# Three modulation tiles moved from the q and k projections to the v projections and the state updates

## The chip, the cores and the metric

The kernel runs on one core of a Trainium2 chip. The metric is the device time of one execution in microseconds (us), as the median of several runs; the kernel before has three runs, 2333.09, 2335.57 and 2336.96 us.

## The reference, cut to what matters

The model is one transformer block with a gated linear attention mixer and a mixture of experts, followed by a second block of other mixers and a plain MLP. The change touches only the beginning of the first block:

```python
mod_x = (jax.nn.silu(c) @ w_ada[l] + b_ada[l])[:, None, :]
sh1, sc1, g1, sh2, sc2, g2 = jnp.split(mod_x, N_MOD, axis=-1)
p_x = modulate(rmsnorm(h, norm_mix_w[l]), sh1, sc1) @ w_in[l]
p_c = modulate(rmsnorm(hc, norm_mix_w[l]), csh1, csc1) @ w_in[l]
# split p into q, k, v, gates, pool; chunked attention over context and tokens
h = h + g1 * (mix_x @ w_out[l])
h = h + g2 * moe(modulate(rmsnorm(h, norm_mlp_w[l]), sh2, sc2), ...)
```

There are 512 tokens and 256 context rows of width 1024. The modulation is a vector of 6 x 1024 values, cut here into 12 tiles of 512. Tiles 0 to 3 are sh1 and sc1 and are needed first. Tiles 4 to 7 are sh2 and sc2, needed only by the expert layer, after this phase. Tiles 8 to 11 are the gates g1 and g2.

## The kernel before, in words

`phase_first` is one block of five engine programs (SyncE, ScalarE, GpSimd, TensorE, VectorE), each a fixed list of instructions in written order, tied by semaphores. No planner chooses the order; it is the order of the calls in the file.

A modulation tile t takes four steps. SyncE loads a 2 MB piece of `w_ada` into a slot of the buffer `W` (`load`, recorded as L249). TensorE multiplies it with the silu of c in 32 small matmuls (`ada(t)`, L435) and raises `mm`. VectorE copies the 128x128 result to `mod_rows` (`row(t)`, L684), which raises `rowd`. TensorE turns it round by one transpose (`spread(t)`, L451), which raises `turn`, and VectorE adds the bias to it and stores it (`col(t)`, L697, and for scale tiles also L702), which raises `cold`. Tiles 4 to 11 all use the one slot 0, the one bank ps3 for `ada` and the one bank ps2 for `spread`. So `spread(t)` waits for `rowd` of t, `ada(t)` for `rowd` of t-1, `row(t)` for `turn` of t-1 and SyncE loads tile t only when `mm` has reached t, that is, when `ada(t-1)` has finished.

The projections are jobs: `project(j)` (L474) is eight matmuls of 512 columns (256 for the context half of k), into ps0 or ps1 in turn, and waits until the job two before it was taken out of its bank. Jobs 0 to 3 are the pool input, 4 to 7 are k (token and context parts), 8 and 9 are q, 10 to 15 are v for six tiles of rows, 16 to 19 are g. ScalarE takes jobs 4 to 15 out (`evict`, L332, semaphore `ev_a`), between large exponentials of the decay: in its order stand evict 4, evict 5, the exponential of `el` (L342), evict 6, two exponentials (L345, L347), evict 7. The exponential of `el` waits for four VectorE subtractions (L832), those of L345 and L347 for four more (L836). Job 8 cannot begin before evict 6, and job 9 not before evict 7.

VectorE's order there is: the scans of the decay (L824, L826), `row(5)`, the L832 subtractions, the L836 subtractions, `col(5)`, `row(6)`, `col(6)`, products with k (L844, L847), `row(7)`, `col(7)`, products with q (L853, L854), then `advance` for state steps 0 to 3 (L726). `update(step)` (L504) is 8 small TensorE matmuls, `turn_k` (L492) four transposes. The profile records each float32 matmul twice (16 for a job, 64 for an `ada`) and each transpose once. After job 15 come `ada(8)` and four rounds of job g, updates, scores, spread and the next `ada` (9 to 11); then the outputs and the projection `out` (L561), and the phase ends.

SyncE's own order matters too, because it is one queue:

```python
for t in range(5, 9):
    sp.wait_ge(mm, t)
    load(0, w_ada(t))
sp.wait_ge(zd, 1)
...
for i in range(fills):
    sp.dma_start(k.y[first + i * P:...], zero...).then_inc(zero_out, 16)
sp.wait_ge(pj, PROJ_V)
load(1, w_cols(a["w_out"], 0, 512))
for t in range(9, 12):
    sp.wait_ge(mm, t)
    load(0, w_ada(t))
```

The 15 fills (L275) write zeros of 512 KB each to `moe_y` in memory. They stand behind the load of tile 8, which waits for `ada(7)`, and ahead of half of `w_out` and of the load of tile 9.

Of the kernel before, what the change touches and what calls it, by code (L numbers as in the profile page):

```python
# [55 lines left out]
class Weights:  # L56
# [24 lines left out]
    def tile(self, n):  # L81
        kk, w = self.jobs[n][1]
        s = self.slot[n]
        return self.buf[:, s * SLOT:s * SLOT + kk * w].rearrange("p (k n) -> p k n", k=kk)
# [65 lines left out]
def phase_first(nc, k, a):  # L150
# [6 lines left out]
    with ExitStack() as st:  # L157
# [71 lines left out]
        def state(d, step):  # L229

            n = order[d][step] if step < NCH else None
            if n is None or n >= XCH:
                return S_ctx[:, step % 2, 2 * d:2 * d + 2, :]
            return S[:, n, 2 * d:2 * d + 2, :]
# [191 lines left out]
        def _(pe):  # L426
            def ada(t):
                pe.wait_ge(slot_in[ADA_HOME[t]], 16 * ADA_TURN[t])
                if 2 <= t < 4:
                    pe.wait_ge(rowd, t - 1)  # L430
                elif t >= 4:
                    pe.wait_ge(rowd, t)
                for kk in range(KD):
                    for q in range(4):
                        last = pe.matmul(ada_bank(t)[32 * q:32 * q + 32, :], narrow[:, kk, :], slot[ADA_HOME[t]][:, kk, tile(q)], start=kk == 0, stop=kk == KD - 1)  # L435
                last.then_inc(mm, 1)

            def spread(t):
                pe.wait_ge(rowd, t + 1)
                if 2 <= t < 4:  # L440
                    pe.wait_ge(cold, t - 1)
                elif t >= 4:
                    pe.wait_ge(cold, t)
                bank = spread_bank(t)
                if gate(t):
                    pe.wait_ge(picked, 5)
                    for q in range(4):
                        last = pe.matmul(bank[:, tile(q)], pick[:, q, :], modr[:, t % 2, :], start=True, stop=True)
                    last.then_inc(turn, 1)
                else:  # L450
                    pe.transpose(bank[:, 0:P], modr[:, t % 2, :], k.ident[:]).then_inc(turn, 1)  # L451
# [10 lines left out]
            def project(j, lo=0, hi=KD):  # L462
                lhs, rhs, n = jobs[j]
                if lo == 0:
                    if 2 <= j < 6:
                        pe.wait_ge(ev_v, j - 1)
                    elif 6 <= j < 18:
                        pe.wait_ge(ev_a, j - 5)
                    elif j >= 18:
                        pe.wait_ge(gmul, j - 17)  # L470
                for kk in range(lo, hi):
                    if j == 0:
                        pe.wait_ge(modx, 2 * kk + 2)
                    last = pe.matmul(ps[j % 2][:, 0:n], lhs(kk), rhs(kk), start=kk == 0, stop=kk == KD - 1)  # L474
                if hi == KD:
                    last.then_inc(pj, 1)
# [10 lines left out]
            def turn_k(n):  # L487
                i = STATE_TILES[n]
                if n >= 2:
                    pe.wait_ge(kdone, n - 1)  # L490
                for q in range(4):
                    last = pe.transpose(ps[4 + n % 2][:, tile(q)], el[:, q, tile(i)], k.ident[:])  # L492
                last.then_inc(tr, 1)

            def update(step):

                if step:
                    pe.wait_ge(sdone, 4 * step)
                for d in range(2):
                    n = order[d][step]  # L500
                    r = halfs[n % 2]
                    for h in range(4):
                        at = (h // 2) * P
                        last = pe.matmul(ps[6 + d][halfs[h % 2], at:at + P], el[r, 2 * d + h // 2, (n // 2) * P + 64 * (h % 2):(n // 2) * P + 64 * (h % 2) + 64],  # L504
                                         v[r, n // 2, h * P:(h + 1) * P], start=True, stop=True)
                last.then_inc(u, 1)
# [97 lines left out]
            spread(4)  # L604
            pe.wait_ge(slot_in[1], 32)
            project(4)
            ada(5)
            project(5)
            project(6)
            spread(5)  # L610
            ada(6)
            project(7)
            project(8)
            spread(6)
            ada(7)
            project(9)
            spread(7)
            pe.wait_ge(v_in, 32)
            project(10)
            project(11)  # L620
            pe.wait_ge(z_v, 1)
            pe.wait_ge(feat, 2)
            turn_k(0)
            turn_k(1)
            project(12)
            pe.wait_ge(kdone, 2)
            update(0)
            project(13)
            update(1)
            turn_k(2)  # L630
            turn_k(3)
            project(14)
# [44 lines left out]
        def _(dve):  # L677
            link = linker(dve, vch)

            def row(t):  # L680
                dve.wait_ge(mm, t + 1)
                if t >= 2:
                    dve.wait_ge(turn, t - 1)
                dve.tensor_copy(modr[:, t % 2, :], ada_bank(t)).then_inc(rowd, 1)  # L684

            def col(t):
                which, half = ADA_COLUMNS[t] // 2, ADA_COLUMNS[t] % 2
                dve.wait_ge(turn, t + 1)
                if gate(t):
                    dve.wait_ge(bg_in, 16 * (t - 7))  # L690
                    i, c = {2: 0, 5: 1}[which], slice(half * 512, half * 512 + 512)
                    dve.tensor_tensor(k.gate_rows[:, i, c], spread_bank(t)[:], bg[:], ALU.add).then_inc(cold, 1)
                    return
                i, f = {0: 0, 1: 1, 3: 2, 4: 3}[which], slice(half * 4, half * 4 + 4)
                src = spread_bank(t)[:, 0:P].rearrange("p (q a r) -> p q a r", q=4, a=2)[:, :, :, 0]
                bias = bcol[:, which * 8 + half * 4:which * 8 + half * 4 + 4].rearrange("p (q o) -> p q o", o=1).to_broadcast([P, 4, 2])
                dve.tensor_tensor(k.modc[:, i, f, :], src, bias, ALU.add).then_inc(cold, 1)  # L697
                if i in (1, 3):
                    name = "norm_mix_w" if i == 1 else "norm_mlp_w"
                    nw = k.vec[:, VEC[name] + half * 4:VEC[name] + half * 4 + 4].rearrange("p (q o) -> p q o", o=1).to_broadcast([P, 4, 2])  # L700
                    dve.wait_ge(cold, t + 1)
                    dve.scalar_tensor_tensor(out=k.modc[:, i, f, :], in0=k.modc[:, i, f, :], scalar=1.0, in1=nw, op0=ALU.add, op1=ALU.mult).then_inc(halfd, 1)  # L702
# [15 lines left out]
            def advance(step):  # L718
                dve.wait_ge(u, step + 1)
                if step >= 1:  # L720
                    dve.wait_ge(sdone, 4 * step)
                for d in range(2):
                    n = order[d][step]
                    for m in range(2):
                        at = m * P
                        dve.scalar_tensor_tensor(out=state(d, step + 1)[:, m, :], in0=state(d, step)[:, m, :], scalar=decay[:, 2 * d + m, n:n + 1],  # L726
                                                 in1=ps[6 + d][:, at:at + P], op0=ALU.mult, op1=ALU.add).then_inc(sdone, 1)
# [95 lines left out]
            for i in range(4):  # L823
                link(dve.scalar_tensor_tensor(out=cum[:, i, :], in0=cum[:, i, :], scalar=0.0, in1=el[:, i, :], op0=ALU.min, op1=ALU.subtract))  # L824
                back = slice(None) if i < 2 else slice(None, None, -1)
                dve.tensor_tensor_scan(cum[:, i, back], scanmask, cum[:, i, back], 0.0, ALU.mult, ALU.add).then_inc(cum_done, 1)  # L826
            row(5)
            dve.wait_ge(cum_done, 4)
            for i in range(4):
                lastp = 63 if i < 2 else 0  # L830
# [2 lines left out]
            for i in range(4):  # L833
                midp = 31 if i < 2 else 32
                cv = cum[:, i, 0:T].rearrange("p (n c) -> p n c", c=CH)
                dve.tensor_tensor(em[:, i, :].rearrange("p (n c) -> p n c", c=CH), cv, cv[:, :, midp:midp + 1].to_broadcast([P, XCH, CH]), ALU.subtract).then_inc(dm, 1)  # L836
            col(5)
            row(6)
            col(6)
            dve.wait_ge(ev_a, 4)  # L840
            dve.wait_ge(ee, 6)
            for d in range(2):
# [2 lines left out]
            for d in range(2):  # L845
                dd = slice(2 * d, 2 * d + 2)
                dve.tensor_tensor(ei[:, dd, :], ei[:, dd, :], kT[:, :, 0:T], ALU.mult).then_inc(feat, 1)  # L847
            row(7)
            col(7)
            dve.wait_ge(ev_a, 6)  # L850
            for d in range(2):
                dd = slice(2 * d, 2 * d + 2)
# [1 line left out]
                dve.tensor_tensor(cum[:, dd, 0:T], cum[:, dd, 0:T], qT, ALU.mult).then_inc(feat, 1)  # L854
            dve.wait_ge(zeroed, 2)
            dve.wait_ge(const_in, 32)
            for step in range(4):
                advance(step)
            row(8)
            for i in range(TT):  # L860
                advance(4 + 2 * i if i < 3 else 10)
# [1870 lines left out]
```

## Time and profile before

| what | value |
|---|---|
| median of 3 runs | 2335.57 us |
| the profiled execution | 2333.08 us |
| its span in the profile | 2331.3 us |
| TensorE busy | 2033.8 us (87%) |
| VectorE busy | 712.5 us (31%) |
| ScalarE busy | 302.7 us (13%) |
| GpSimd busy | 261.3 us (11%) |

The span is from the first to the last recorded instruction. Busy time is an average over stages with different limits: the first phase, where the change is, ends at about 307 us of the span, and the expert layer and the second block take the rest. PE is TensorE, PEld its weight loads, DVE VectorE, ACT ScalarE, POOL GpSimd, SPq the queue of SyncE. PEclk is the TensorE clock that was granted, as a share of full speed (2.4 GHz); 0.50 is 1.2 GHz.

### The profile page before, as it was taken

What the parts mean: (1) busy time and instruction counts of PE and PEld (TensorE: products, weight loads), DVE (VectorE), ACT (ScalarE), POOL (GpSimd) and SP (SyncE); (2) the same over time, 40 slices, a digit from 0 to 9 for tenths busy, and PEclk for the clock granted to TensorE, in tenths of its full rate; (3) what the DMA queues carried; (4) which work ended last, traced back from release to release, by engine and by line L of the source; (5) the groups of instructions that cost most, each with busy time, mean ns of one, the idle gap of its engine ahead of it and who ended that gap; (6) DMA issues with size and microseconds to landing.
All of it is one profiled execution on the core that took longest, in us unless ns stands there. A gap on an engine that the chain in (4) does not pass through costs nothing. (4 is left out here: it accounts for less than half of the span.)

```text
span 2331.3 us, 41450 instructions
## 1 busy us (share of the span) xinstructions
PE 2033.8 (87%) x17359; PEld 983.8 (42%) x17359; DVE 712.5 (31%) x1352; ACT 302.7 (13%) x599; POOL 261.3 (11%) x290
## 2 busy tenths in 40 slices
PE   5899962999799999989899870999987989999998
PEld 3445550443233443434243320447674434444443
DVE  2633241332122332322232226484555210100002
ACT  2320130000000000000000001332232100000001
POOL 2920003110001110101011003002200000000000
PEclk9999966999899999999899985999987999999999
DMA  9463265999999999999999995100101422112000
GB/s 367 158 207 123 73 241 212 413 409 418 420 418 418 419 418 418 419 418 418 418 418 418 419 374 194 48 0 1 60 3 43 183 72 72 72 72 81 36 0 36
DMA packets 138093, 548.44 MB, mean 235 GB/s; under 512 B 19658, under 2 KB 40670, under 8 KB 88578
## 3 DMA queue, kind: packets, MB, share of 16 engines
q1 hardware_dynamic: 113904, 514.60, 55.0%
q0 software_dynamic: 7104, 19.18, 2.2%
q10 hardware_dynamic: 16946, 12.54, 1.7%
q8 instruction: 120, 1.97, 0.3%
q14 instruction: 19, 0.16, 0.0%
HBM read 523.54 MB, written 22.71 MB: 234 GB/s over the span
## 5 line engine op out<-in xcount | busy, mean ns | idle before, releaser
L1241 PE MATMUL ps<-W,x_modulated 128*32 128x512 f32 x3168 | 384.7, 625 | 90.2 <-DVE x_modulated L1319 41.7
L1241 PE MATMUL ps<-W_high,x_modulated 128*32 128x512 f32 x2016 | 238.6, 612 | 29.4 <-DMA W_high<-in_w_gu 23.4
L1241 PEld LDWEIGHTS ps<-W,x_modulated 128*32 128x32 f32 x3168 | 108.3, 112 | 329.0 <-issue 186.1
L2621 PE MATMUL ps<-hT,W 128*128 128x512 f32 x512 | 223.1, 596 | 3.3 <-PE ps L2621 2.0
L2659 PE MATMUL ps<-W,hid 128*128 128x512 f32 x512 | 221.6, 593 | 2.7 <-PEq L2603 1.7
L1328 DVE TENSOR_SCALAR gate<-ps 128x256 f32<-128x256 f32 x81 | 34.3, 424 | 604.4 <-PE ps L1245 604.4
L1257 PE MATMUL ps<-W,hidden_turned 128*32 128x256 f32 x3200 | 183.3, 380 | 1.1 <-DVE hidden_turned L1339 1.1
L2621 PEld LDWEIGHTS ps<-hT,W 128*128 128x128 f32 x512 | 97.2, 191 | 128.7 <-issue 128.7
L2659 PEld LDWEIGHTS ps<-W,hid 128*128 128x128 f32 x512 | 96.7, 190 | 127.7 <-issue 127.7
L1639 PE MATMUL ps<-hT,W 128*128 128x512 f32 x336 | 146.5, 594 | 1.9 <-PEq L1434 1.6
L1257 PEld LDWEIGHTS ps<-W,hidden_turned 128*32 128x32 f32 x3200 | 117.5, 110 | 69.3 <-issue 16.1
L1241 PEld LDWEIGHTS ps<-W_high,x_modulated 128*32 128x32 f32 x2016 | 71.3, 111 | 172.3 <-issue 120.2
L1282 ACT ACTIVATE sig<-gate 128x256 f32<-128x256 f32 x81 | 33.8, 417 | 694.9 <-DVE gate L1328 694.9
L1212 POOL COPY rows_idx<-slot_rows 128x1 int32 (+1 forms) x82 | 22.6, 275 | 829.7 <-DVE x_turned L1315 824.8
L1257 PE MATMUL ps<-W_high,hidden_turned 128*32 128x256 f32 x1984 | 114.6, 382 | 0.0
L1639 PEld LDWEIGHTS ps<-hT,W 128*128 128x128 f32 x336 | 63.3, 190 | 81.6 <-issue 81.4
L1257 PEld LDWEIGHTS ps<-W_high,hidden_turned 128*32 128x32 f32 x1984 | 71.4, 111 | 46.0 <-issue 12.4
L1215 POOL DMA_INDIRECT x_rows<-moe_xn,rows_idx x82 | 80.2, 978 | 64.5 <-POOL rows_idx L1212 64.5
L2639 DVE TENSOR_TENSOR hid<-relu_tmp 128x512 f32<-128x512 f32 x32 | 22.1, 691 | 204.8 <-ACT relu_tmp L2633 204.8
L474 PE MATMUL ps<-hT,W 128*128 128x512 f32 (+1 forms) x160 | 65.9, 567 | 7.6 <-DMA W<-in_w_in 4.0
L2559 PE MATMUL ps<-W,mixT 128*128 128x512 f32 x128 | 58.4, 616 | 14.0 <-PEq L1994 13.9
L1339 DVE STREAM_TRANSPOSE hidden_turned<-hidden 128x256 f32<-128x256 f32 x81 | 36.1, 445 | 106.9 <-ACT y_rows L1289 106.8
(531 smaller groups left out, 1972.6 us busy)
## 6 DMA issues: line engine op xcount, KB each, us to landing
W<-in_w_gu SPq DMA_DIRECT2D x152, 1024.0 KB
W_high<-in_w_gu SPq DMA_DIRECT2D x104, 1024.0 KB
W<-in_w_down SPq DMA_DIRECT2D x80, 1024.0 KB
W_high<-in_w_down SPq DMA_DIRECT2D x48, 1024.0 KB
W<-in_mlp_w SPq DMA_DIRECT2D x16, 2048.0 KB, 8.7
W<-in_w_ada SPq DMA_DIRECT2D x12, 2048.0 KB
W<-in_w_in SPq DMA_DIRECT2D x9, 2048.0 KB, 18.3
moe_y<-y_rows ACTq DMA_DIRECT2D x324, 32.0 KB
```

Source lines behind the costliest of these rows:

```text
L474: last = pe.matmul(ps[j % 2][:, 0:n], lhs(kk), rhs(kk), start=kk == 0, stop=kk == KD - 1)
L1212: pool.tensor_copy(rows_idx[:], m.idx4[:, bass.ds(u, 1)]).then_inc(idx_set, 1)
L1215: pool.indirect_dma_start(xg[:], None, m.xn, bass.IndirectOffsetOnAxis(ap=rows_idx[:, 0:1], axis=0)).then_inc(x_in, 16)
L1241: last = pe.matmul(gu_out(j), xs[:, kk, :], quarter(ex.view(n), j), start=kk == 0, stop=False)
L1257: last = pe.matmul(down_bank[SUB * j:SUB * (j + 1), 0:256], hT[:, kk, :], ex.view(n)[:, kk % 2, j * 256:(j + 1) * 256], start=kk == 0, sto ...
L1282: act.activation(sig[:], gate[:], ACT.Sigmoid, scale=1.702).then_inc(sigd, 1)
L1328: dve.tensor_scalar(gate[:], gu_bank[:, 0:256], SWIGLU_LIMIT, None, ALU.min).then_inc(gated, 1)
L1339: dve.transpose(hT[:].rearrange("p k t -> p (k t)"), hid[:]).then_inc(h_ready, 1)
L1639: last = pe.matmul(ps[j % 4][:, 0:nn], lhs(kk), rhs(kk), start=kk == 0, stop=kk == KD - 1)
L2559: last = pe.matmul(ps[2 * i + half][:], mixT[:, kk, i * P:(i + 1) * P], w.tile(O2 + half)[:, kk, :], start=kk == 0, stop=kk == KD - 1)
L2621: last = pe.matmul(ps[j % 8][:], w.tile(n)[:, kk, (j % 4) * P:(j % 4 + 1) * P], hT[:, kk, :], start=kk == 0, stop=kk == KD - 1)
L2659: last = pe.matmul(ps[2 * i + half][:], hid[:, 4 * g + q, i * P:(i + 1) * P], w.tile(L + g)[:, q, half * 512:(half + 1) * 512], start=g == ...
```

## The change

On TensorE, `ada` and `spread` of tiles 5, 6 and 7 leave the stretch between jobs 4 and 10. `ada(5)` now stands after job 10 and `spread(5)` after job 11; `ada(6)` after `turn_k(1)` and `spread(6)` after job 12; `ada(7)` after `update(0)` and `spread(7)` after `update(1)`. On VectorE the `row` and `col` calls of these tiles leave the decay and product steps and stand ahead of and between `advance(0)` and `advance(2)`. SyncE's list is not edited, nor ScalarE's, nor GpSimd's.

```diff
             project(4)
-            ada(5)
             project(5)
             project(6)
-            spread(5)
-            ada(6)
             project(7)
             project(8)
-            spread(6)
-            ada(7)
             project(9)
-            spread(7)
             pe.wait_ge(v_in, 32)
             project(10)
+            ada(5)
             project(11)
+            spread(5)
             pe.wait_ge(z_v, 1)
             pe.wait_ge(feat, 2)
             turn_k(0)
             turn_k(1)
+            ada(6)
             project(12)
+            spread(6)
             pe.wait_ge(kdone, 2)
             update(0)
+            ada(7)
             project(13)
             update(1)
+            spread(7)
             turn_k(2)
             turn_k(3)
...
-            row(5)
             dve.wait_ge(cum_done, 4)
...
-            col(5)
-            row(6)
-            col(6)
             dve.wait_ge(ev_a, 4)
             dve.wait_ge(ee, 6)
...
-            row(7)
-            col(7)
             dve.wait_ge(ev_a, 6)
...
             dve.wait_ge(const_in, 32)
-            for step in range(4):
-                advance(step)
+            row(5)
+            col(5)
+            row(6)
+            col(6)
+            advance(0)
+            row(7)
+            advance(1)
+            col(7)
+            advance(2)
+            advance(3)
             row(8)
```

## Rows read from the trace of the kernel before

**Rows 1.** Busy time by stretch; columns: stretch, length, PE, PEld, DVE, ACT, POOL, PEclk, DMA share, GB/s.
```profile
97.70:136.30 38.60, 24.54 (x180) 14.13 (x179) 32.70 (x22) 10.60 (x10) 29.90 (x17) 0.87 0.39 133
136.30:304.30 168.00, 167.12 (x1025) 86.22 (x1025) 48.35 (x119) 19.12 (x58) 5.13 (x4) 1.00 0.35 122
```

**Rows 2.** TensorE in time order: start, duration, engine, line, work, [idle before, releaser].
```profile
85.25 1.95 PE L435 MATMUL ps<-W,silu_narrow 128*32 128x128 f32 x64
87.13 10.59 PE L474 MATMUL ps<-hT,W 128*128 128x256 f32 x32
105.33 0.47 PE L451 MATMUL ps<-ident,mod_rows 128*128 128x128 f32 x1 [7.61 <-DVE mod_rows L684]
105.73 3.64 PE L435 MATMUL ps<-W,silu_narrow 128*32 128x128 f32 x64
...
115.36 7.13 PE L474 MATMUL ps<-hT,W 128*128 128x512 f32 x16 [2.01 <-ACT kT L332]
124.20 0.33 PE L451 MATMUL ps<-ident,mod_rows 128*128 128x128 f32 x1 [1.70 <-DVE mod_rows L684]
...
128.08 7.13 PE L474 MATMUL ps<-hT,W 128*128 128x512 f32 x16 [1.67 <-ACT kT L332]
136.28 0.33 PE L451 MATMUL ps<-ident,mod_rows 128*128 128x128 f32 x1 [1.07 <-DVE mod_rows L684]
136.45 3.61 PE L474 MATMUL ps<-W,hT 128*128 128x512 f32 x8
```

**Rows 3.** VectorE in time order, the same stretch.
```profile
105.01 0.26 DVE L684 COPY mod_rows<-ps 128x128 f32<-128x128 f32 x1
105.19 6.83 DVE L832 TENSOR_TENSOR W<-W 128x768 f32<-128x768 f32 x4
111.95 11.91 DVE L836 TENSOR_TENSOR W<-W 128x512 f32<-128x512 f32 x4
```

**Rows 4.** ScalarE in time order, the same stretch.
```profile
112.06 2.76 ACT L342 ACTIVATE W<-W 128x3072 f32<-128x3072 f32 x1 [19.49 <-DVE W L832]
114.73 0.58 ACT L332 ACTIVATE kT<-ps 128x512 f32<-128x512 f32 x1
...
127.66 0.36 ACT L332 ACTIVATE kT<-ps 128x256 f32<-128x256 f32 x1
```

**Rows 5.** TensorE in time order, v jobs to the first g round.
```profile
143.33 3.60 PE L474 MATMUL ps<-W,hT 128*128 128x512 f32 x8
...
150.19 1.04 PE L492 MATMUL ps<-ident,W 128*128 128x128 f32 x8
...
158.03 0.68 PE L504 MATMUL ps<-h,W 64*64 64x128 f32 x16
158.64 3.70 PE L474 MATMUL ps<-W,hT 128*128 128x512 f32 x8
...
183.52 1.96 PE L435 MATMUL ps<-W,silu_narrow 128*32 128x128 f32 x64
185.40 2.84 PE L474 MATMUL ps<-W,hT 128*128 128x512 f32 x6
...
196.06 1.95 PE L435 MATMUL ps<-W,silu_narrow 128*32 128x128 f32 x64
```

**Rows 6.** SyncE's queue in time order: start, time over which the group was issued.
```profile
126.88 24.02 SPq L275 DMA_DIRECT2D moe_y<-y_zero  x15
150.94 1.43 SPq L249 DMA_DIRECT2D W<-in_w_out  x1
185.53 0.37 SPq L249 DMA_DIRECT2D W<-in_w_ada  x1
```

**Rows 7.** The end of the backlog behind the fills, by stretch (last column GB/s).
```profile
161.00:162.00 1.00, 1.00 (x4) 0.46 (x3) 0.00 (x0) 0.00 (x0) 0.00 (x0) 1.00 0.19 72
162.00:163.00 1.00, 1.00 (x3) 0.38 (x2) 0.00 (x0) 0.00 (x0) 0.00 (x0) 1.00 0.08 31
163.00:164.00 1.00, 1.00 (x4) 0.48 (x3) 0.00 (x0) 0.00 (x0) 0.00 (x0) 1.00 0.00 0
```

**Rows 8.** DMA issues of 2129 to 2145, then 2150 to 2170: KB, us to landing.
```profile
W<-in_mlp_w SPq DMA_DIRECT2D x1, 2048.0 KB, 8.7
...
W<-in_mlp_w SPq DMA_DIRECT2D x1, 2048.0 KB, 7.5
```

**Rows 9.** TensorE earlier in the phase: a pool job after an idle gap, and one without.
```profile
42.23 8.57 PE L474 MATMUL ps<-hT,W 128*128 128x512 f32 x16 [3.95 <-DMA W<-in_w_in]
...
61.39 7.13 PE L474 MATMUL ps<-hT,W 128*128 128x512 f32 x16
```

**Rows 10.** The first of these two by stretch (PEclk is the third from last).
```profile
42.00:43.00 1.00, 0.77 (x1) 0.50 (x2) 0.00 (x0) 0.00 (x0) 0.00 (x0) 0.50 0.94 378
```

## The prediction

> **What bounds the kernel now.** I read busy time by stretch first. From 97.7 to 136.3 us TensorE is busy for 24.5 of 38.6 us: this is a stretch with holes, 14.1 us of them. From 136.3 to 304.3 it is busy for 167.1 of 168.0 us at the full clock: there TensorE is the path, and every microsecond of work put in it is a microsecond of the kernel's time [rows 1]. GpSimd has nearly nothing there, and VectorE is idle for more than two thirds of it, so they can give nothing back. The phase ends when TensorE's last `out` and its residual are done, and the expert layer begins behind that; I found no later work tied to an absolute time.
>
> Then TensorE in time order shows what ends each hole: 7.61 us before `spread(5)`, 2.01 before job 8, 1.70 before `spread(6)`, 1.67 before job 9 and 1.07 before `spread(7)` [rows 2]. They are of two kinds. The three before a spread are ended by a `row` copy, the two before a job by ScalarE's evictions. VectorE and ScalarE in time order show where those come from. The L832 subtractions run from 105.19 to 112.02, the exponential of `el` starts at 112.06, evict 6 at 114.73, and job 8 starts at 115.36. The L836 subtractions end at 123.86, evict 7 stands behind two exponentials at 127.66, and job 9 starts at 128.08 [rows 2 to 4]. This decay chain (VectorE, then ScalarE, then the jobs) sets the time of jobs 8 and 9, whatever TensorE does in between. The three `ada` sat in its holes.
>
> **What is removed.** `row(5)` stood ahead of the L832 subtractions. Its copy lasts 0.26 us, and the subtractions started 0.18 us after it [rows 3]. With it gone, jobs 8 and 9 can begin some 0.15 us earlier. `col(5)`, `row(6)`, `col(6)` and `row(7)`, `col(7)` came behind the L836 subtractions, and VectorE then waits for ScalarE anyway; their removal gives nothing. So job 9 starts at about 127.9, and the stall ahead of it grows. Jobs 5 to 7 close up: job 4 ends at 85.3, and two jobs of 256 columns (3.5 each) and one of 512 (7.0) end at 99.4. TensorE then waits until about 115.2 for evict 6, 15.8 us in one piece; job 8 follows, and another hole stays ahead of job 9.
>
> What is gained is behind job 9. Job 10 started 8.37 us after job 9 (136.45 less 128.08); a job of 512 columns alone takes 7.03 (7.13 recorded, less the overlap with the next), so 1.34 us of waiting for `row(7)` and of `spread(7)` goes [rows 2]. Together with the 0.15: **1.5 us gained**.
>
> **What is added on the path.** Three `ada` from start to next start are 87.13 less 85.25 = 1.88 us each, 5.64 together; three spreads at 0.17 us each (136.28 to 136.45) are 0.5 [rows 2]. All six now stand behind job 10, where TensorE has no hole. **6.1 us added, 4.6 net.** The `row` copies (0.26 each) and `col` sums of this tile group land on VectorE when it is idle; TensorE's spreads wait for a row a whole job earlier. `advance(0)` waits behind `col(6)`, which waits for `spread(6)`, 0.6 us ahead of `update(0)`'s end; `update(1)` asks for `advance(0)` a job (7 us) later, and `advance` takes about 1 us. Hidden; if that cover were gone it would cost some 1 us a step.
>
> **The loads of tiles 6 and 7.** SyncE loads tile 6 only when `ada(5)` has ended. Before, there was time; now `ada(6)` follows after job 11 (6.86), a spread (0.17) and two turns (0.88), 7.9 us, and `ada(7)` after job 12 (158.03 less 150.19, less those turns: 6.96), a spread and `update(0)` (0.61), 7.7 us [rows 5]. Two lone 2 MB loads landed 8.7 and 7.5 us after their issue, which is 0.1 us after the semaphore [rows 8]. By the one end 0.9 and 1.1 us of waits arise, by the other nothing; I take the middle, **0.7 us together**, and keep 0 to 2.0.
>
> **The load of tile 9, the part that is easily overlooked.** The 15 fills wait for the load of tile 8, and that for `ada(7)`. `ada(7)` ended at about 126.4; it will end at about 164, and the queue behind it moves with it, not by 4 us but by 37. From the issue of the fills SyncE needs 24.0 us for them and 1.4 for half of `w_out` [rows 6], and the last bytes moved at 163.0, 36.6 us after `ada(7)` [rows 7]. Before, `ada(9)` had that behind it long since: its own load was issued at 185.53, behind an empty queue. Now `ada(8)` ends 185.4 less 158.64 = 26.8 us after `ada(7)` does, plus `spread(7)`, so tile 9 is issued 27.0 us after `ada(7)`, and its 2 MB stand behind a backlog that ends at 36.6. At the 400 GB/s of such loads they need 5.2 us more: landing 41.8 us after `ada(7)`. If the tail of the backlog (72 and 31 GB/s at 161 and 162) is of one slow engine and the others go on at once, it is 161.2 + 5.4, or 40.2 us. TensorE asks for it 196.06 less 158.64 plus a spread = 37.6 us after `ada(7)` [rows 5]. So `ada(9)` waits 2.6 to 4.8 us (if the fills also slow down a little); I take **4.0 us**. Who waits behind it: the second g job, and so everything to the end of the phase. Tiles 10 and 11 keep their 12.5 us distance and an empty queue, and cost nothing.
>
> What the sum rests on here is that one queue serves its transfers in order. The Trainium skill (DMA: Bandwidth & Descriptors, section "Queues, rings and completion order") says that on each DMA engine descriptors are consumed in ring order, and that SyncE owns one such row of rings. The row agrees so far as it goes: 7.9 MB of fills took 24.0 us to issue, 330 GB/s, so the queue was full and held SyncE [rows 6]. By a rule of fair sharing instead, the load would land about 8 us after its issue, before it is asked for at 10.6, and the term would be zero; that is the first rival.
>
> **The clock.** After a hole of 7.61 us `ada(6)` took 3.64 us where `ada(5)` took 1.95 [rows 2]; after one of 3.95 us a pool job took 8.57 us where 7.13 is usual, with a granted clock of 0.50 of the 2.4 GHz, so 1.2 GHz [rows 9, 10]. Holes of 2.01, 1.70 and 1.67 us left no trace. Job 8 will start at half clock after 15.8 us of idling and lose about 2.2 us (what `ada(6)` and job 7 lost), hidden in the hole ahead of job 9: it ends at about 124.5 instead of 122.2. The hole that is left ahead of job 9 is 3.4 to 5.7 us, and the one ahead of `ada(9)` about 4.0. Both are like the 3.95 one, whose price was 8.57 less 7.13 = 1.4 us; the bounds for each are 0 (as after 2.01) and 2.2. I take **1.4 for job 9 and 1.0 for `ada(9)`**.
>
> **Sum.** +4.6 (work moved onto the path) + 0.7 (tiles 6, 7) + 4.0 (tile 9) + 2.4 (clock) = +11.7 us. Against the profiled execution, 2333.08 us (span 2331.3 and 1.8 around it), that is 2344.8. The median of the runs shown is 2.5 us above the profiled one; the measured time is a median too, so I add 11.7 to something between the two and say 2346 us.
>
> **Rivals.** (1) *Only the moved work and the clock count* (12 in 100): the loads arrive in time, because the queue does not hold tile 9 back (above). For it: I have no row with a load queued behind fills. Against: all of it is one queue, and the margin is small only if the backlog drains faster than before. Then +4.6 + 0.7 + about 1.4 = +6.7, 2341.5 us; with no clock loss either +4.6, 2339.5, hardly to be told from no change.
>
> (2) *The decay chain shrinks by more than the copy* (7 in 100), which ends on the other side. The L836 subtractions take 11.91 us for four, 3.0 each, and the longer L832 ones 6.83, 1.7 each [rows 3]: a tile of 512 columns takes longer than one of 768, while GpSimd is busy in 29.9 of 38.6 us [rows 1]. Something outside VectorE stretches them. If taking the copies and sums away shifted VectorE against GpSimd so that the four ran at the 768-column rate, job 9 would start 11.91 - 6.83 = 5.1 us earlier, and the net of moved work would be -0.5; with holes too short for the clock or the loads to matter it could be 2335. It decides from about 5 us of a shift. Against it: 0.15 us of shift, with GpSimd's own chain unchanged, is little to do so.
>
> (3) *Both holes at `ada(9)` and job 9 are deep* (18 in 100): loads of tiles 6 and 7 wait their full 2.0, tile 9 4.8, and both clock losses are 2.2: +4.6 + 2.0 + 4.8 + 4.4 = +15.8, 2350 us.
>
> **Numbers.** My forecast, +9 to +14 us, has 63 in 100, rival 1 12, rival 2 7, rival 3 18. Range: 2339.5 (rival 1 without a clock loss) to 2351 (rival 3 and a us of spread). A measurement of this kernel tells about 0.2%, 4.7 us, from no change; half of rival 2 and a fifth of rival 1 fall within it or in the spread of runs. Faster 0.03, same 0.07, slower 0.90.
>
> **What would show it.** In the new profile: one hole of 15 to 16 us ended by ScalarE's eviction before job 8, at 115; job 9 at 127.9, and job 10 seven to eight and a half us behind; `ada(6)`, `ada(7)` released by a DMA with under 1.2 us of waiting each; `ada(9)` released by a DMA after 2.6 to 4.8; fills issued from about 165; granted clock 0.50 in parts of 116 to 132 and about 205. The prediction is wrong if job 9 starts more than 1 us from 127.9, if `ada(9)` has no wait ahead of it, or if a hole later in the phase takes the delay up.

## The result and the profile after

| | before | changed |
|---|---|---|
| median | 2335.36 us (4 runs) | 2351.86 us (4 runs) |
| lowest to highest | 2333.09 to 2336.96 | 2348.24 to 2354.36 |
| profiled execution, its span | 2333.08, 2331.3 | 2352.40, 2350.6 |

The ratio is 1.007 (95% interval 1.0053 to 1.0088): the changed kernel is slower, by 16.5 us. Forecast were 2346 us and a range up to 2351.0; the result stands 0.9 us outside it. The changed kernel was measured again later, in five runs (the last experiment), at 2347.62 us, a ratio of 1.006 (1.0046 to 1.0074).

TensorE of the changed kernel in time order, the stretch that answers to [rows 2] and the end of [rows 5] (start, duration, engine, line, work, idle before and its releaser):

```profile
80.15 0.27 PE L451 MATMUL ps<-ident,mod_rows 128*128 128x128 f32 x1
...
117.31 8.56 PE L474 MATMUL ps<-hT,W 128*128 128x512 f32 x16 [16.25 <-ACT kT L332]
130.03 8.83 PE L474 MATMUL ps<-hT,W 128*128 128x512 f32 x16 [4.16 <-ACT kT L332]
138.70 3.60 PE L474 MATMUL ps<-W,hT 128*128 128x512 f32 x8
142.13 3.60 PE L474 MATMUL ps<-gate_rows,hT 128*128 128x512 f32 x8
145.66 1.96 PE L435 MATMUL ps<-W,silu_narrow 128*32 128x128 f32 x64
...
154.62 1.04 PE L492 MATMUL ps<-ident,W 128*128 128x128 f32 x8
155.72 1.95 PE L435 MATMUL ps<-W,silu_narrow 128*32 128x128 f32 x64
...
165.75 1.95 PE L435 MATMUL ps<-W,silu_narrow 128*32 128x128 f32 x64 [0.29 <-DMA W<-in_w_ada]
167.63 3.70 PE L474 MATMUL ps<-W,hT 128*128 128x512 f32 x8
...
210.12 3.64 PE L435 MATMUL ps<-W,silu_narrow 128*32 128x128 f32 x64 [4.89 <-DMA W<-in_w_ada]
213.69 3.87 PE L474 MATMUL ps<-W,hT 128*128 128x512 f32 x6
217.50 0.68 PE L504 MATMUL ps<-h,W 64*64 64x128 f32 x16
```

The five small holes are now two, 16.25 us ahead of job 8 and 4.16 ahead of job 9, both ended by ScalarE's evictions. Nothing waits for a row copy any more, and there are two new waits, for the load of tile 7 (0.29) and for that of tile 9 (4.89). Behind the holes the same work takes longer: job 9 and the step to job 10 last 8.67 us, `ada(9)` 3.64 where it took 1.95, and the six records of the g job 3.87 where they took 2.84.

SyncE's queue of the changed kernel, to be set beside [rows 6]:

```profile
168.18 23.62 SPq L275 DMA_DIRECT2D moe_y<-y_zero  x15
191.84 1.41 SPq L249 DMA_DIRECT2D W<-in_w_out  x1
194.63 0.96 SPq L249 DMA_DIRECT2D W<-in_w_ada  x1
```

The fills are issued at 168 instead of 127. Tile 9 is issued 15.5 us ahead of `ada(9)`, where it had been 10.5 us ahead, and still comes late.

Busy time by stretch (columns as in [rows 1]); the first two lines answer to its two, the others are single microseconds at job 9 and at the end of the wait for tile 9:

```profile
101.00:138.70 37.70, 17.30 (x34) 7.29 (x33) 30.42 (x16) 9.99 (x9) 28.59 (x16) 0.73 0.00 0
138.70:321.05 182.35, 176.25 (x1220) 93.13 (x1218) 49.75 (x125) 19.77 (x59) 5.10 (x4) 0.98 0.44 152
131.00:132.00 1.00, 1.00 (x2) 0.34 (x1) 0.00 (x0) 1.00 (x1) 0.00 (x0) 0.50 0.00 0
209.00:210.00 1.00, 0.00 (x0) 0.00 (x0) 0.00 (x0) 0.00 (x0) 0.00 (x0) 0.50 0.14 55
208.00:209.00 1.00, 0.00 (x0) 0.00 (x0) 0.00 (x0) 0.00 (x0) 0.00 (x0) 0.99 0.72 260
```

The holes grew from 14.1 to 20.4 us, and the stretch behind them, which was full, now lasts 182.4 us instead of 168.0. The granted clock falls to 0.50 (1.2 GHz) while TensorE waits for tile 9, at 209, and job 9 runs a part of its time at it.

**A yardstick for the experiments.** Not all of the difference between two traces is the change. The first pool job took 8.57 us in the trace of before [rows 9] and 8.9 to 10.0 us in the ten others, though nothing ahead of it differs: the half clock behind its wait lasts longer or shorter. So I read each trace from the start of `spread(4)`, the last step ahead of every edit, to the expert layer's first transpose, which depends on the end of this phase. These are the two ends in the kernel before and in the changed one:

```profile
78.17 0.27 PE L451 MATMUL ps<-ident,mod_rows 128*128 128x128 f32 x1
...
319.46 6.42 PE L1043 MATMUL ps<-ident,xn_tok 128*128 128x128 f32 x32 [15.19 <-DVE xn_tok L1066]
```

```profile
336.24 6.55 PE L1045 MATMUL ps<-ident,xn_tok 128*128 128x128 f32 x32 [15.19 <-DVE xn_tok L1068]
```

That is 241.29 us before and 336.24 - 80.15 = 256.09 changed: the change costs 14.8 us in its own stretch. All kernels by this yardstick, and by their medians against that of before in the same runs. The last column is the ratio on record, which is close to the quotient of the two medians but not the same:

| kernel | stretch, us | against before | median, us | before, us | ratio (95%) |
|---|---|---|---|---|---|
| before | 241.29 | 0 | | | |
| changed | 256.09 | +14.8 | 2351.86 | 2335.36 | 1.007 (1.0053 to 1.0088) |
| changed, again | 255.42 | +14.1 | 2347.62 | 2334.58 | 1.006 (1.0046 to 1.0074) |
| fills early | 248.12 | +6.8 | 2344.16 | 2334.98 | 1.0037 (1.0022 to 1.0051) |
| holes filled | 251.61 | +10.3 | 2346.23 | 2334.98 | 1.0042 (1.0029 to 1.0055) |
| tile 7 only | 250.06 | +8.8 | 2343.69 | 2334.98 | 1.0037 (1.0019 to 1.0055) |
| fills early, holes filled | 248.01 | +6.7 | 2340.56 | 2335.37 | 1.002 (1.0009 to 1.0031) |
| before, two evictions early | 241.04 | -0.3 | 2333.16 | 2335.37 | 0.9987 (0.9978 to 0.9997) |
| changed, fills and evictions early | 238.11 | -3.2 | 2331.18 | 2334.98 | 0.9983 (0.9972 to 0.9995) |
| the same, k product and row(5) early | 225.49 | -15.8 | 2320.73 | 2335.37 | 0.9936 (0.9919 to 0.9953) |
| evictions early, tiles not moved | 224.05 | -17.2 | 2317.42 | 2335.37 | 0.9918 (0.9901 to 0.9934) |

Of the ten executions of "changed, fills and evictions early" two were slow (3118 and 3612 us, granted clocks of 0.65 and 0.56); they are in its median of 2331.18, the other eight have 2330.65, and no ratio counts them.

### The profile page after: what moved, and what is told of

Read it like the earlier page. It is cut to its first block and busy times, and to the rows that moved or that the text cites. A ratio compares the mean times of both kernels' runs of the same rounds, so it can differ in the third digit from the quotient of the medians.

```text
span 2350.6 us, 41450 instructions
## 1 busy us (share of the span) xinstructions
PE 2042.9 (87%) x17359; PEld 983.8 (42%) x17359; DVE 713.2 (30%) x1352; ACT 302.8 (13%) x599; POOL 261.0 (11%) x290
## 5 line engine op out<-in xcount | busy, mean ns | idle before, releaser
L474 PE MATMUL ps<-hT,W 128*128 128x512 f32 (+1 forms) x160 | 69.5, 594 | 24.8 <-ACT kT L332 20.4
```

## The experiments

**Fills early.**

```diff
-            for t in range(5, 9):
+            sp.wait_ge(mm, 5)
+            load(0, w_ada(5))
+            # the 15 fills
+            for t in range(6, 9):
                 sp.wait_ge(mm, t)
                 load(0, w_ada(t))
-            # the 15 fills
```

> The changed kernel, with one edit on SyncE: the 15 fills are issued right behind the load of tile 5 instead of behind that of tile 8. Theory (the queue holds tile 9 back behind the fills and TensorE cools while it waits): the 4.9 us wait ahead of ada(9) and the 2.7 us at half clock behind it go, 7.6 us, so about 2344.3 where the changed kernel has 2351.9, and half a microsecond or so of clock spread. Rival (the wait at ada(9) is of another cause, or the fills cost as much elsewhere): 2350 to 2354, with the wait still there or a new one at tile 6.

Measured: 2344.16 us, 7.7 below the changed kernel's first median and 3.5 below its second; by the stretch, where both traces can be compared piece by piece, 8.0 and 7.3. TensorE in its trace:

```profile
116.29 9.76 PE L476 MATMUL ps<-hT,W 128*128 128x512 f32 x16 [16.25 <-ACT kT L334]
129.00 8.53 PE L476 MATMUL ps<-hT,W 128*128 128x512 f32 x16 [2.96 <-ACT kT L334]
164.43 1.95 PE L437 MATMUL ps<-W,silu_narrow 128*32 128x128 f32 x64 [0.30 <-DMA W<-in_w_ada]
...
203.84 1.95 PE L437 MATMUL ps<-W,silu_narrow 128*32 128x128 f32 x64
```

`ada(9)`, at 203.84, has no wait ahead of it and runs in 1.95 us. All that was moved are the fills in SyncE's list; so the late tile 9 is theirs, and no new wait took its place. The first rival of the prediction, that the queue does not hold tile 9 back, falls. Which rule of the queue does it is not shown: between the issue and the landing of tile 9 in the changed kernel 5.1 MB moved, 3.0 of them not its own, and that delay would come from strict order and from a shared rate alike.

**Holes filled.** This kernel, and the later one with the holes filled, add matmuls whose results are overwritten unread; nothing is left out.

```diff
+            def keep_busy(n):
+                for _ in range(n):
+                    pe.matmul(ps[3][:], hT[:, 0, tile(0)], hT[:, 0, 0:T], start=True, stop=True)
...
             project(7)
+            keep_busy(16)
             project(8)
+            keep_busy(5)
             project(9)
...
+                if i == 0:
+                    keep_busy(4)
                 if i < 3:
                     ada(9 + i)
```

> The changed kernel, with idle TensorE time filled by matmuls whose result nobody reads: 16 ahead of job 8, 5 ahead of job 9, 4 ahead of ada(9) (each about 0.88 us). No wait is taken away. Theory (the half clock behind the holes costs 1.6 us at job 9 and 2.7 us at ada(9)): 4.3 us less than the changed kernel, 2347.6, job 10 starting 7.0 to 7.1 us after job 9 instead of 8.7. Rival (the clock is a label without cost here, the excess is spread between executions): no change, 2351.9, or up to 1 us slower through matmuls that end late.

Measured: 2346.23 us; the stretch is 4.5 us shorter than the changed kernel's, against 4.3 expected. The medians say 5.6 against the first and 1.4 against the second of the changed kernel, so they alone would not carry it; the records do:

```profile
115.94 7.13 PE L478 MATMUL ps<-hT,W 128*128 128x512 f32 x16 [2.53 <-ACT kT L332]
128.65 7.13 PE L478 MATMUL ps<-hT,W 128*128 128x512 f32 x16 [1.28 <-ACT kT L332]
...
202.04 3.60 PE L440 MATMUL ps<-hT 128*128 128x512 f32 x8
206.96 1.96 PE L435 MATMUL ps<-W,silu_narrow 128*32 128x128 f32 x64 [1.32 <-DMA W<-in_w_ada]
208.84 2.84 PE L478 MATMUL ps<-W,hT 128*128 128x512 f32 x6
```

Both q jobs take 7.13 us, `ada(9)` 1.96 and the g records behind it 2.84. The semaphores wait as before (jobs 8 and 9 start 37.2 and 49.9 us after `spread(4)`, as they did), but each stretch of work behind them runs at full clock. The half clock is a price of its own, beside the waits.

**Tile 7 only.** On the kernel before, `ada(7)`, `spread(7)`, `row(7)` and `col(7)` alone go where the changed kernel has them.

```diff
             spread(6)
-            ada(7)
             project(9)
-            spread(7)
...
             update(0)
+            ada(7)
             project(13)
             update(1)
+            spread(7)
```

> The kernel before, with tile 7 alone moved to where the changed kernel has it (tiles 5 and 6 stay between the k and q jobs). Theory by terms: one ada and one spread more behind job 10 and the 1.24 us ahead of job 10 gone, net +0.9; the whole wait for tile 9, +4.9, and its clock, +2.7, since the fills hang on tile 7 alone; a hole of 3.6 us ahead of job 9 that may cost up to 1.6: +8.5 to +10, so 2344 to 2345.5. Rival (time goes in proportion to the tiles moved): a third of +16.5, 2341.

Measured: +8.7 us by the medians, +8.8 by the stretch, where a third of the change would be 5.

```profile
125.63 0.33 PE L451 MATMUL ps<-ident,mod_rows 128*128 128x128 f32 x1 [1.70 <-DVE mod_rows L684]
129.51 8.80 PE L474 MATMUL ps<-hT,W 128*128 128x512 f32 x16 [3.55 <-ACT kT L332]
...
204.68 3.54 PE L435 MATMUL ps<-W,silu_narrow 128*32 128x128 f32 x64 [4.86 <-DMA W<-in_w_ada]
208.15 2.84 PE L474 MATMUL ps<-W,hT 128*128 128x512 f32 x6
```

The whole wait for tile 9, 4.86 us, comes with tile 7 alone. The other two tiles add 4.9 us ahead of `ada(9)`: their steps and joints, and 0.3 us of waiting for a load. The clock price at `ada(9)` was 1.6 us here and 2.7 in the changed kernel behind nearly the same wait: the g records were at full clock again.

**Changed, with fills and evictions early.** If the evictions gate, freeing them must make the moved order pay. The fills stand as in the first experiment; on ScalarE:

```diff
             evict(4, k_out[0])
             evict(5, k_out[1])
+            evict(6, k_out[2])
+            evict(7, k_out[3])
+            evict(PROJ_Q, qT[:, 0, :], 64.0 ** -0.5)
             act.wait_ge(dl, 4)
             act.activation(el, el, ACT.Exp, scale=1.0 / 16.0).then_inc(ee, 1)
-            evict(6, k_out[2])
+            evict(PROJ_Q + 1, qT[:, 1, :], 64.0 ** -0.5)
+            evict(PROJ_V, v[:, STATE_TILES[0], :])
             act.wait_ge(dm, 4)
...
-            evict(7, k_out[3])
```

> The changed kernel with the fills early (as in the first run), and ScalarE's evictions 6, 7 and 8 moved ahead of the exponential of el, 9 and 10 ahead of the two exponentials behind it. Theory (jobs 8 and 9 wait for nothing but evictions that stand behind exponentials in ScalarE's order): TensorE runs jobs 4 to 11 without a hole, then waits some 4 us for the products with k ahead of the first turns; ada(6) starts about 21 us earlier than in the changed kernel; with 7.6 for the fills 2323 to 2325, below both kernels. Rival (VectorE's products or the decay chain gate just behind, the hole only moves to the turns): the turns start no earlier than 150, and 2338 to 2344.

Measured: 2331.18 us, below both kernels, but 6 to 8 us above what I expected.

```profile
79.68 34.54 PE L478 MATMUL ps<-hT,W 128*128 128x512 f32 x96
114.05 3.60 PE L478 MATMUL ps<-W,hT 128*128 128x512 f32 x8
...
126.43 3.60 PE L478 MATMUL ps<-gate_rows,hT 128*128 128x512 f32 x8
141.99 0.48 PE L455 MATMUL ps<-ident,mod_rows 128*128 128x128 f32 x1 [11.95 <-DVE mod_rows L688]
```

Jobs 4 to 11 run without a hole, so the evictions were the gate. Then 11.95 us are lost ahead of `spread(5)`: it waits for `row(5)`, which the change has put behind all products with q. I had counted on the turns as the next gate and overlooked the copy. Half clock comes behind this hole too: `ada(6)` took 2.83 us instead of 1.95. In the changed kernel this place of `row(5)` is harmless only because job 10 is so late: the products with q end at 144.2 there, and `spread(5)` is due at 154.5.

**Before, with two evictions early.** Only evictions 6 and 7 go ahead of the exponential, on the kernel before.

> The kernel before, with ScalarE's evictions 6 and 7 moved ahead of the exponential of el, and nothing else. Theory: jobs 8 and 9 lose their waits (2.0 and 1.7 us), but spread(5), spread(6) and spread(7) still wait for row copies that stand behind the scans, the subtractions and the products, so job 10 starts where it did, about 136.5: no change, 2334 to 2336. Rival (the evictions alone gate the stretch): job 10 up to 3.7 us earlier, 2331.

Measured: 2333.16 us, 2.2 below before, while the stretch is 0.3 shorter.

```profile
125.54 0.33 PE L451 MATMUL ps<-ident,mod_rows 128*128 128x128 f32 x1 [3.42 <-DVE mod_rows L684]
125.80 3.38 PE L435 MATMUL ps<-W,silu_narrow 128*32 128x128 f32 x64
...
137.37 0.33 PE L451 MATMUL ps<-ident,mod_rows 128*128 128x128 f32 x1 [0.92 <-DVE mod_rows L684]
```

The eviction waits are gone. The wait for the copy ahead of `spread(6)` (3.42 for the 1.70 of [rows 2]) and half clock behind it (`ada(7)` 3.38 us for 1.95) have taken them over; `spread(7)` starts 57.9 us after `spread(4)`, against 58.1. The theory holds in the trace. That the medians differ by 2 us I cannot place in this stretch; it stays open.

**Fills early and holes filled.** Both of the earlier edits, but for the four matmuls ahead of `ada(9)`.

> The changed kernel with the fills early and with 16 and 5 unread matmuls in the holes ahead of jobs 8 and 9. This leaves of the change only the moved work on the path and the small wait at ada(7). Theory: 1.6 us below the kernel with the fills early (2344.2), 2342.6, and +6 to +7.5 over the kernel before, of which the trace should show 7.0 between job 10 and ada(9), 0.3 of it a load wait, and 1.3 taken off between jobs 9 and 10. Rival (the clock costs nothing at job 9): 2344.2.

Measured: 2340.56 us, +5.2 (the interval allows 2 to 7), stretch +6.7. Job 10 starts 6.97 us after job 9, as expected. But the 1.4 us won there went nearly whole into the wait ahead of `ada(7)`:

```profile
165.26 1.95 PE L437 MATMUL ps<-W,silu_narrow 128*32 128x128 f32 x64 [1.60 <-DMA W<-in_w_ada]
```

The load of tile 7 can begin only when `ada(6)` has ended, and its landing varies from one execution to the next. Here it came 9.3 us after the issue, in the changed kernel's second trace 8.0; the waits behind the same code were 0.29 to 1.60 us.

**The same with the k product and row(5) early.** On the kernel with fills and evictions early, VectorE's product of `el` with k waits for the first exponential alone, and `row(5)` stands behind it.

```diff
             dve.wait_ge(ev_a, 4)
-            dve.wait_ge(ee, 6)
+            dve.wait_ge(ee, 1)
             # products of el with k
+            row(5)
+            dve.wait_ge(ee, 6)
             # products of ei with k, then with q
-            row(5)
             col(5)
```

> The kernel with the fills and the evictions early, and on VectorE the products of el with k and row(5) straight behind the L836 subtractions, ahead of the wait for the last exponentials. Theory (what was left in the earlier one was a hole of 11.95 us ahead of spread(5), ended by row(5), which stood behind the products with q): TensorE runs without a hole of over 1 us from job 4 to the outputs; ada(6) starts at about 131 to 132 where it started at 144.1; 2331.2 less 12 to 13.5: 2317.5 to 2319. Rival (another gate close behind, at the turns or at update(0)): 2322 to 2328.

Measured: 2320.73 us, 1.7 above what was expected, 14.6 below before. TensorE's only waits in the stretch are 1.01 us at `spread(5)`, 0.33 at `ada(7)` and 0.61 and 0.25 near the outputs.

**Evictions early, tiles not moved.** On the kernel before, with the evictions and the product of k as above, the fills where they were, and the three tiles between the k and q jobs.

```diff
                 dve.tensor_tensor_scan(cum[:, i, back], ...)
+                if i == 0:
+                    row(5)
+                if i == 2:
+                    col(5)
+                    row(6)
...
             # L832 subtractions
+            col(6)
+            row(7)
             # L836 subtractions
-            col(5)
-            row(6)
-            col(6)
```

> The tile move undone in the kernel with early evictions: tiles 5 to 7 back between the k and q jobs, the fills in their old place in SyncE's list, evictions 6 to 10 and the products of el with k early, row(5) between the scans, row(6) behind the third scan, row(7) behind the L832 subtractions. Theory (where the tiles stand has no worth of its own once the evictions do not gate; what counts is that no copy or eviction waits behind work it does not need): same work without holes, so within 2 us of the run with tiles moved. Rival (the moved place is the better one, its copies are out of the decay chain): 3 us or more above that run; VectorE's chain is at most 0.8 us longer by three copies.

Measured: 2317.42 us, ratio 0.9918 (0.9901 to 0.9934), the fastest of all, 18.0 us below before and 3.3 below the version with the tiles moved (1.4 by the stretch). By the stretch it is within the 2 us expected, by the medians it is not, and in both it differs the other way from the rival. The 1.4 us of the stretch are nearly the two waits that only the moved version has (1.01 and 0.33); the rest of the 3.3 between the medians, of four executions each, is not placed. Its own stretch, busy time from job 6 to job 10 and from there to near the phase's end:

```profile
97.70:121.10 23.40, 23.40 (x184) 13.37 (x183) 23.26 (x16) 5.62 (x5) 22.53 (x13) 1.00 0.52 172
121.10:287.00 165.90, 165.04 (x1022) 85.53 (x1021) 61.12 (x126) 25.60 (x64) 14.39 (x10) 1.00 0.37 130
```

TensorE is never idle up to job 10 and idle for 0.9 us in the 166 behind it, at full clock throughout. With the evictions and the copies no longer behind work that they do not need, the old place of the tiles costs nothing. How much of the 17.2 us each of these moves gives by itself was not measured.

**The changed kernel again.**

> The changed kernel again, unedited, beside the kernel before, for the size of the loss and its spread. By the terms read between the end of job 4 and the end of the phase in the two traces the change costs 14.8 us; the medians differ by 16.5. If the 1.7 us between them is spread between executions (the first pool job, ahead of the change, took 8.57 us in the trace of before and 8.9 to 10.0 in all others), the medians should now differ by 14 to 16 us, and the trace again show the same terms to within 1 us each, but for the two clock losses, which may move by 1 us. If something later in the kernel adds to it, 16.5 or more.

Measured: 2347.62 us, 13.0 above before (10.7 to 17.3 by the interval), stretch +14.1. Its trace:

```profile
116.17 9.77 PE L474 MATMUL ps<-hT,W 128*128 128x512 f32 x16 [16.27 <-ACT kT L332]
128.89 8.53 PE L474 MATMUL ps<-hT,W 128*128 128x512 f32 x16 [2.95 <-ACT kT L332]
...
164.31 1.95 PE L435 MATMUL ps<-W,silu_narrow 128*32 128x128 f32 x64 [0.37 <-DMA W<-in_w_ada]
...
208.59 3.64 PE L435 MATMUL ps<-W,silu_narrow 128*32 128x128 f32 x64 [4.79 <-DMA W<-in_w_ada]
212.16 3.57 PE L474 MATMUL ps<-W,hT 128*128 128x512 f32 x6
```

Every wait is within 0.1 us of the first trace, but the one ahead of job 9, where job 8 took 9.77 us instead of 8.56 and left less to wait. The stretch and this median agree within a microsecond or so; the first median's further 1.7 us do not come back.

## Why the prediction was wrong, step by step

The direction and the four terms were right; three sizes were too small (the half clock at `ada(9)` above all, then the wait ahead of it and the joints), and the upper end of the range left no room for the spread of a median on top. By the two traces of the changed kernel, between `spread(4)` and the end of the phase:

| term | forecast | first trace | second trace |
|---|---|---|---|
| job 9 starts later | -0.15 | 0.0 | 0.0 |
| job 9 to job 10, with its clock price | +0.06 | +0.3 | 0.0 |
| three `ada`, three spreads and their joints | +6.1 | +6.6 | +6.6 |
| waits for the loads of tiles 6 and 7 | +0.7 | +0.3 | +0.4 |
| wait for the load of tile 9 | +4.0 | +4.9 | +4.8 |
| half clock behind that wait | +1.0 | +2.7 | +2.4 |
| sum, before rounding | +11.7 | +14.8 | +14.1 |

*The failed step is the clock at `ada(9)`.* The prediction took 1.0 us because the price of the 3.95 us hole was 1.4 [rows 9] and such holes sometimes cost less. From the start of `ada(9)` over the six g records behind it to the start of `update(6)` it is 217.50 - 210.12 = 7.38 us; before, it was 200.72 - 196.06 = 4.66. The price of 2.7 us is more than even the upper bound of 2.2 that the prediction took from what `ada(6)` and job 7 lost. The row of the first pool job was a poor base: 8.57 us was the least of eleven traces, the others had up to 9.97, a price of 2.8 by the same sum. One execution shows one draw of it, and I read it as the size. Filling the hole took the price away, which shows that it is the clock.

*The wait for tile 9* came at the upper end of its bounds of 2.6 to 4.8, 0.1 us beyond it in the first trace. The landing came at 210.1, 42.5 us after `ada(7)` ended at 167.6, where 41.8 and 40.2 were the two readings. So the tail of the backlog counted in full or nearly; I had leaned to the middle. The prediction's 8 us for a shared queue left out the 3.0 MB of other transfers still to be moved and was no price for the first rival.

*The joints*: each `ada` was priced at 1.88, start to next start, but setting one between two jobs also lengthens what follows it. The two turns last 1.10 us to the next start instead of 0.88, and a job behind an `ada` shows 3.70 in its first half instead of 3.60. Three insertions made 0.5 us. A part of the 1.10 may be a wait for the load of tile 6 too short to be listed: it was 0.99 to 1.10 in the traces with this code.

*The moved work itself* came as worked out. Filling the late holes and moving the fills leaves +6.7, the moved steps less what job 10 had waited for, plus a load wait. VectorE and ScalarE ran as forecast: the subtractions took 6.88 and 11.92 us against 6.83 and 11.91 [rows 3], and so the second rival, a decay chain that shrinks, falls. `advance` stayed hidden. The 0.15 us that job 9 was to gain did not come: the L832 subtractions began 0.08 us earlier by the yardstick and lasted 0.05 longer.

*The signs of being wrong.* The prediction called itself wrong if job 9 started more than 1 us from 127.9, and the trace has it at 130.03. That is no fault of the mechanism: `spread(4)`, ahead of every edit, started 2.0 us later too, and from there to job 9 it is 49.88 us against 49.91. The sign should have been set from such a step and not in time of the span. The other two did not come: `ada(9)` waited, and no later hole took the delay up.

*Slips in the working.* The fills move by 39 us by the prediction's own terms, not 37 (39.3 measured from `spread(4)`); nothing hangs on it, since the wait was counted from `ada(7)`. The 4.8 is not one of its two readings, which give 2.6 and 4.2, but an allowance for slower fills. And the sum and rival 3 stand on a kernel before of 2334.3 us, rival 1 on 2334.8.

*The third rival*, all terms deep, was nearest to the first median (2350 against 2351.9), and the forecast to the second (2346 against 2347.6). What the range lacked was the spread of the measurement beside the bounds of the terms: two medians of one kernel lay 4.2 us apart, and I had given it one microsecond. That the first median fell outside at all is in part chance: 14.8 us on the prediction's 2334.3 are 2349.1, inside the range, as is the second median. The size of the clock term was wrong in either case.

*What the prediction did not ask* is why jobs 8 and 9 were gated. It took the decay chain for the cause because it ended the waits. The chain ended them only since two short evictions, whose jobs were done at about 98 and 101 us of the changed kernel's trace, stood in ScalarE's list behind exponentials that could not start before 114:

```profile
114.01 2.76 ACT L342 ACTIVATE W<-W 128x3072 f32<-128x3072 f32 x1 [21.54 <-DVE W L831]
116.68 0.58 ACT L332 ACTIVATE kT<-ps 128x512 f32<-128x512 f32 x1
125.85 1.91 ACT L345 ACTIVATE W<-W 128x2048 f32<-128x2048 f32 x1 [8.59 <-DVE W L835]
127.80 1.91 ACT L347 ACTIVATE W<-W 128x2048 f32<-128x2048 f32 x1
129.61 0.37 ACT L332 ACTIVATE kT<-ps 128x256 f32<-128x256 f32 x1
```

Freeing the evictions is worth 10.0 us of the stretch in the changed kernel (238.11 against 248.12, both with the fills early) and 0.3 in the kernel before, where the copies gate next. Only with the copies and the product with k freed as well do the two last kernels gain 15.8 and 17.2 us over the kernel before, more than the change lost.

## What to carry to other kernels

A step moved out of a stretch with holes into a full one costs its whole length and leaves the holes; first ask what ends each hole, and whether the releasing instruction itself waits or only stands behind one that does. Follow each moved step to every semaphore that counts it, above all in queues that the diff does not touch: here 15 transfers hung on the last of three steps, moved by 41 us and made a fourth tile late. And price a hole twice, once as idle time and once as half clock behind it, with bounds from several such places rather than from one.

## What the runs showed of the hardware

The half clock behind a hole varies between executions of the same code: behind 3.1 to 4.6 us of waiting, the first pool job took 8.57 to 9.97 us in eleven traces, where 7.13 is the full-clock time. It does not follow the length of the wait: 3.09 us of waiting came with 9.32, 4.61 with 8.97. Behind 16.3 us of waiting job 8 took 8.56 us in one execution and 9.77 in the other. And the wait for tile 7 behind a lone 2 MB load was 0.29, 0.30, 0.37, 0.45 and 1.60 us in five traces, in which the load was issued at the same point of TensorE's work.
